# Seven half-block products for an eight-product up projection, alternating with the down projection

## The chip, the cores and the metric

The kernel runs on one core of one Trainium2 chip. The metric is device time in microseconds (us) of one execution of the whole program, as the median of several runs. In the profile PE is the matmul engine (TensorE), PEld its weight loads, DVE is VectorE, ACT ScalarE, POOL GpSimd, and SP the engine whose queue issues most transfers.

## The reference, cut to what matters

One block of a first kind is followed by two layers of a second kind. The change touches only the feed-forward of those two layers, over 512 tokens, a model width of 1024 and a hidden width of 4096, all in float32:

```
u = rms_norm(h, g_mlp) @ w_ff1              # (512, 1024) @ (1024, 4096)
h = h + jnp.square(jax.nn.relu(u)) @ w_ff2  # (512, 4096) @ (4096, 1024)
```

## The kernel before, in words

Activations are kept transposed: features on the 128 partitions, the 512 tokens along the free dimension. To keep float32 accuracy, every operand is split into a high part (rounded to the fast matmul format) and a low part (the rest), and every product is three matmuls: high x high, high x low and low x high. `xh` and `xl` are the split activations of the up product, `n.U` those of the down product.

A weight tile is 1024 rows by 256 columns (1 MB, 8 KB in each partition). SP loads the tiles in the order of `W.tiles` into `ring`, which has two slots (`NSLOT`). A load waits until both halves of the tile two places earlier have been split (`load`, L738). ACT copies a half to its high part (`high_half`, L1465), POOL subtracts to get the low part in four instructions of 128x256 (`low_half`, L2900). `wh` and `wl` hold two tiles' halves. PE's `product` (L795) makes one output tile of 128 features x 512 tokens from one half: 8 blocks of rows x 3 matmuls (L808 to L810), in one of the eight PSUM banks.

Which half is split ahead of which product is decided by `Weights.plan`: before each product it adds up to three halves whose place in `wh` and `wl` is free. Every engine then runs its own program in a fixed order; a wait at its head holds everything behind it.

The feed-forward of a layer has four groups of 1024 hidden features, each eight up products and eight down products, in the order up 0, up 1, down 0, up 2, down 1, up 3, down 2, down 3. Behind an up product DVE takes relu and the norm factor (L2574), ACT squares to the high part (L1781), DVE squares (L2576) and subtracts for the low part (L2578). Behind a down product DVE adds to `h` (L2586).

## Time and profile before

| | us |
|---|---|
| median of 3 runs | 2062.11 |
| lowest and highest | 2060.41 to 2064.62 |
| span of the profiled execution | 2057.3 |
| PE busy | 2013.4 |
| DVE, POOL, ACT busy | 1135.5, 917.4, 867.9 |

The span runs from the first to the last instruction of the program in one profiled execution. That execution's own device time is not recorded apart from it; 2062.11 less 2057.3 leaves 4.8 us around the span. A busy matmul is a pipelined record: neighbouring ones overlap, so the pace is read from their start times and not from their durations. The other engines' records are real stretches of work, save that the next may start some 0.08 us before the last one ends.

### The profile page before, as it was taken

The page shows a single profiled execution, that of the slowest core. Times are in us where ns is not written, and L with a number is a line of the kernel's source. Part 1 is how long each engine was busy: PE and PEld are TensorE (multiplying, and loading weights), DVE is VectorE, ACT ScalarE, POOL GpSimd, SP SyncE. Part 2 cuts the span into 40 slices and gives each one's busy share as a digit, 9 for nine tenths or more (in the row PEclk, how much of TensorE's full clock was granted, in tenths as well). Part 3 has the DMA queues.
Part 4 walks back from the last instruction along what each step waited for, and adds up shares of the span by engine and source line. Part 5 has one row for each costly group of instructions (what it writes and reads, how often), then busy time and mean ns, then how long its engine had stood idle before and what let it go on. Part 6 is the DMA issues. An engine that isn't in the chain of part 4 may idle for free.

```text
span 2057.3 us, 26250 instructions
## 1 busy us (share of the span) xinstructions
PE 2013.4 (98%) x10148; PEld 1574.5 (77%) x10148; DVE 1135.5 (55%) x2020; ACT 867.9 (42%) x1381; POOL 917.4 (45%) x1157
## 2 busy tenths in 40 slices
PE   6999999999999999999999999999999999999998
PEld 2877676888888767768888888786776788888877
DVE  5366758988393579955522231466996543222235
ACT  4542434443233556784322222445578532222242
POOL 1344205876566325541555555302355155555540
PEclk9999999999999999999999999999999999999999
DMA  9034631322323211103333323322111332332331
GB/s 328 25 108 143 217 123 50 105 94 80 121 84 102 89 42 42 62 21 123 92 103 103 99 86 103 102 69 83 42 42 42 103 97 98 103 103 83 102 102 62
DMA packets 188299, 194.26 MB, mean 94 GB/s; under 512 B 8592, under 2 KB 184080, under 8 KB 187792
## 3 DMA queue, kind: packets, MB, share of 16 engines
q1 hardware_dynamic: 187600, 189.44, 28.5%
q10 hardware_dynamic: 576, 3.15, 0.4%
q8 instruction: 81, 1.33, 0.3%
q14 instruction: 42, 0.34, 0.1%
HBM read 190.48 MB, written 2.10 MB: 94 GB/s over the span
## 4 chain that ended last, share of the span: by engine, by line
PE 88%; DVE 6%; POOL 2%; ACT 2%; DMA 1%; issue 1%; SPq 0%; DVEq 0%; ACTq 0%; POOLq 0%
PE ps L808 20%; PE ps L810 20%; PE ps L809 20%; PE ps L827 3%; PE ps L829 3%; PE ps L828 3%; PE ps L855 2%; POOL wl L2900 1%; DVE mix L2512 1%; PE ps L844 1%; PE ps L845 1%; PE ps L846 1%; PE ps L1355 1%; PE ps L1428 1%; PE ps L1411 1%; PE ps L1374 1%
## 5 line engine op out<-in xcount | busy, mean ns | idle before, releaser
L2900 POOL TENSOR_TENSOR wl<-ring,wh 128x256 fp32r<-128x256 f32 x1008 | 754.2, 783 | 807.5 <-ACT wh L1465 807.2
L1465 ACT ACTIVATE wh<-ring 128x1024 fp32r<-128x1024 f32 (+1 forms) x298 | 309.0, 1044 | 311.1 <-PE ps L810 256.9
L808 PE MATMUL ps<-xh,wh 128*128 128x512 f32 (+1 forms) x976 | 383.1, 393 | 2.6 <-POOL wl L2900 2.6
L810 PE MATMUL ps<-xh,wl 128*128 128x512 f32 (+1 forms) x976 | 380.6, 390 | 0.0
L809 PE MATMUL ps<-xl,wh 128*128 128x512 f32 (+1 forms) x976 | 380.6, 390 | 0.0
L808 PE MATMUL ps<-acts,wh 128*128 128x512 f32 x880 | 343.5, 390 | 0.7 <-POOL wl L2900 0.4
L810 PE MATMUL ps<-acts,wl 128*128 128x512 f32 x880 | 342.4, 389 | 0.0
L809 PE MATMUL ps<-acts,wh 128*128 128x512 f32 x880 | 342.4, 389 | 0.0
L2512 DVE SCALAR_TENSOR_TENSOR mix<-ps,par,mix 128x441 f32<-128x441 f32 (+2 forms) x352 | 213.7, 687 | 29.3 <-ACT mix L1712 29.3
L808 PEld LDWEIGHTS ps<-xh,wh 128*128 128x128 f32 (+1 forms) x976 | 183.0, 188 | 47.0 <-issue 9.1
L810 PEld LDWEIGHTS ps<-xh,wl 128*128 128x128 f32 (+1 forms) x976 | 183.0, 187 | 39.4
L809 PEld LDWEIGHTS ps<-xl,wh 128*128 128x128 f32 (+1 forms) x976 | 182.9, 187 | 38.9 <-issue 0.7
L808 PEld LDWEIGHTS ps<-acts,wh 128*128 128x128 f32 x880 | 165.2, 188 | 37.5 <-issue 3.1
L809 PEld LDWEIGHTS ps<-acts,wh 128*128 128x128 f32 x880 | 165.2, 188 | 34.5 <-issue 0.2
L810 PEld LDWEIGHTS ps<-acts,wl 128*128 128x128 f32 x880 | 165.2, 188 | 34.4
L2586 DVE TENSOR_TENSOR h<-h,ps 128x512 f32<-128x512 f32 x64 | 44.0, 688 | 254.2 <-PE ps L810 254.2
L1781 ACT ACTIVATE acts<-mix 128x512 fp32r<-128x512 f32 x64 | 40.5, 632 | 235.0 <-DVE mix L2574 235.0
L2574 DVE SCALAR_TENSOR_TENSOR mix<-ps,arena_f 128x512 f32<-128x512 f32 x64 | 44.2, 690 | 147.3 <-PE ps L810 147.3
L827 PE MATMUL ps<-xh,wh 128*128 128x512 f32 x224 | 92.9, 415 | 0.0
L1470 ACT ACTIVATE arena_m<-ps 128x512 f32<-128x512 f32 (+4 forms) x150 | 66.5, 485 | 62.0 <-PE ps L855 25.5
L829 PE MATMUL ps<-xh,wl 128*128 128x512 f32 x224 | 87.7, 391 | 0.0
L828 PE MATMUL ps<-xl,wh 128*128 128x512 f32 x224 | 87.4, 390 | 0.0
(443 smaller groups left out, 3031.4 us busy)
## 6 DMA issues: line engine op xcount, KB each, us to landing
ring<-in_w_ff_dram SPq DMA_DIRECT2D x64, 1024.0 KB, 5.2
ring<-in_w_in_dram SPq DMA_DIRECT2D x28, 1024.0 KB, 5.0
ring<-in_ffn_w_up_dram SPq DMA_DIRECT2D x22, 1024.0 KB, 4.9
ring<-in_w_ada_dram SPq DMA_DIRECT2D x17, 1024.0 KB, 5.0
ring<-in_w_out_dram SPq DMA_DIRECT2D x12, 1024.0 KB, 5.1
ring<-in_ffn_w_down_dram SPq DMA_DIRECT2D x8, 1024.0 KB, 5.0
ring<-in_w_ple_gate_dram SPq DMA_DIRECT2D x8, 1024.0 KB, 5.0
early<-in_w_ada_dram SPq DMA_DIRECT2D x7, 1024.0 KB, 10.8
```

What stands on the lines that cost most here:

```text
L808: t.matmul(b[0:m, 0:n], s.hi[:, k, a:a + m], x2[0][:, k, :], start=k == ks[0], stop=False)
L809: t.matmul(b[0:m, 0:n], s.hi[:, k, a:a + m], x2[1][:, k, :], start=False, stop=False)
L810: i = t.matmul(b[0:m, 0:n], s.lo[:, k, a:a + m], x2[0][:, k, :], start=False, stop=k == ks[-1])
L827: t.matmul(b[:, :], s.hi[:, k, a:a + 128], x2[0][:, k, :], start=k == ks[0], stop=False)
L828: t.matmul(b[:, :], s.hi[:, k, a:a + 128], x2[1][:, k, :], start=False, stop=False)
L829: i = t.matmul(b[:, :], s.lo[:, k, a:a + 128], x2[0][:, k, :], start=False, stop=k == ks[7])
L1465: a.activation(s.hi[:, :, c], s.ap[:, :, c], ACT.Copy).then_inc(*up("hi", "hi", name, hf))
L1470: a.activation(o, ps(key)[:, :] if i is None else i, func, **kw).then_inc(*free(key))
L2512: k = v.scalar_tensor_tensor(o, grid(ps(key)[:, :], dr, dc, True), pc("ffn_conv_w", w * 44 + col), o, ALU.mult, ALU.add)
L2574: v.scalar_tensor_tensor(u, ps(key)[:, :], 0.0, n.rs2, ALU.max, ALU.mult).then_inc(*free(key))
L2586: v.tensor_tensor(h[:, j, :], h[:, j, :], ps(key)[:, :], ALU.add).then_inc(*free(key))
L2900: i = p.tensor_tensor(s.lo[:, k:k + 2, c], s.ap[:, k:k + 2, c], s.hi[:, k:k + 2, c].bitcast(F32), ALU.subtract)
```

## The change

The first up group of each layer stays as it is. In the other three groups, the 1024 x 256 weights of output tiles i and i+4 are laid out on the host as a 2 x 2 of blocks: half of the rows x one output tile. The activations are a 2 x 2 of half of the rows x half of the tokens. The product of these two 2 x 2 matrices is made with seven block products in place of eight, which needs sums and differences of the blocks on both sides. A block product (a part) is 4 blocks of rows x 3 matmuls of 256 columns.

The four sums of activations are made once for each layer, during the first up group (`turned`). The sums of weights are made for each tile by DVE, in place in the ring slot, in three steps (`sums`): step 2 from the loaded tile, step 3 once the low part of part 0 is made, step 4 once that of part 1 is. The low parts of parts 1 and 4 are DVE's, the other five POOL's. The results come out in four banks, which DVE combines behind parts 2, 4 and 6 (ACT copies bank 0 out first). The order becomes: up group 0, then for each of the first three down groups four times "seven parts, two down products", then down group 3. `wh` and `wl` are now eight places, of which a seven tile takes seven and a down tile four.

The planner's rule, followed for this order, puts the splits of a pair in these places: the high copies of parts 4, 5 and 6 ahead of part 0; both halves of the down tile ahead of part 4; part 0 of the next tile ahead of part 5; part 1 of it, with steps 2 and 3 of its sums, ahead of part 6; its parts 2 and 3 ahead of the first down product; step 4 ahead of the second.

```diff
+SEVEN_RAW = (0, 1, None, 0, 1, 3, 2)
+SEVEN_X = ((0, 0), (1, 0), 1, 2, (1, 1), 3, 0)
+SEVEN_BANK = ((0, 0), (1, 0), (1, 1), (2, 0), (2, 1), (3, 0), (3, 1))
+SEVEN_WHO = ("pool", "vec", "pool", "pool", "vec", "pool", "pool")
+SEVEN_SUMS = (2, 3, 4)
+SEVEN_SUM_OF = {2: 2, 3: 3, 4: 4, 6: 2}
...
+        if seven:
+            t.parts = 7
+        n = 8 if seven else 4 * split
+        t.places = [(self.place + i) % 8 for i in range(n)] if split else [self.place % 8]
+        self.place += n
...
+            spots = self.named[name].spots(hf)
+            self.before[name, hf] = sorted({held[x] for x in spots if x in held} - {(name, hf)}, key=order.index)
+            held.update({x: (name, hf) for x in spots})
...
+                soon = first[name] < n
+                self.sum_at.setdefault(self.uses[n - soon][0], ([], []))[soon].append((name, hf))
...
+                        for p in range(b.parts):
+                            e.wait_ge(*at("lo", b.name, p))
...
+                        (q, u), x, bank = SEVEN_BANK[p], SEVEN_X[p], (*name, "bank", SEVEN_BANK[p][0])
+                        use((*name, p), name, (p,), who="pool")
+                        if u == 0:
+                            take(bank, keep=True, where=None)
+                        b = ps(bank)[:, 256 * u:256 * u + 256]
+                        e.wait_ge(*at("lo", name, p))
+                        if type(x) is int:
+                            e.wait_ge(*at("suml", l, x))
+                            x2 = n.sums[x]
+                        else:
+                            x2 = [y[:, 4 * x[0]:4 * x[0] + 4, 256 * x[1]:256 * x[1] + 256] for y in (xh, xl)]
+                        for k in range(4):
+                            hi, lo = [y[:, 128 * k:128 * k + 128] for y in (s.hi[p], s.lo[p])]
+                            t.matmul(b, hi, x2[0][:, k, :], start=k == 0, stop=False)
+                            t.matmul(b, hi, x2[1][:, k, :], start=False, stop=False)
+                            j = t.matmul(b, lo, x2[0][:, k, :], start=False, stop=k == 3)
+                        j.then_inc(*(full(bank) if q == 0 or u else up("used", "used", *name, p)))
+                        if q == 0 or u:
+                            banks.drop(bank)
+
...
+                for g in range(3):
+                    for i in range(4):
+                        seven(g + 1, i)
+                        down(g, 2 * i)
+                        down(g, 2 * i + 1)
+                for j in range(8):
...
+                for b in W.before[name, hf]:
+                    e.wait_ge(*over(W.through[b][0]))
+                if s.seven and hf in SEVEN_SUM_OF:
+                    e.wait_ge(*at("sum", name, SEVEN_SUM_OF[hf]))
+                a.activation(s.high[hf], s.raw[hf], ACT.Copy).then_inc(*up("hi", "hi", name, hf))
...
+                def seven(g, i):
+                    name = ("ff1", l, g, i)
+                    for p in range(7):
+                        high((*name, p))
+                        if p == 0:
+                            if (g, i) != (1, 0):
+                                e.wait_ge(*taken(("ff1", l, *((g, i - 1) if i else (g - 1, 3)), "bank", 1)))
+                            out_of((*name, "bank", 0), n.copied, ps((*name, "bank", 0))[:, 0:256])
+                    for u in range(2):
+                        j = i + 4 * u
+                        e.wait_ge(*at("relu", l, g, j))
+                        if j == 0:
+                            e.wait_ge(*(at("suml", l, 3) if g == 1 else done(("ff2", l, g - 2, 7))))
+                        a.activation(n.U[g % 2][0][:, j, :], n.uu[2 * (i % 2) + u], ACT.Square).then_inc(*up("act", "u2h", l, g, j))
...
+            def sums(name, p):
+
+                s = W.named[name]
+                q = s.quarter
+                if p == 2:
+                    e.wait_ge(*at("load", name))
+                    v.tensor_tensor(q[2], q[2], q[3], ALU.add).then_inc(*up("vec"))
+                    if name in W.seven_before:
+                        e.wait_ge(*at("lo", W.seven_before[name], 2))
+                    after()
+                    v.tensor_tensor(s.raw[2], q[2], q[0], ALU.subtract).then_inc(*up("vec", "sum", name, 2))
+                elif p == 3:
+                    e.wait_ge(*at("lo", name, 0))
+                    after()
+                    v.tensor_tensor(q[0], q[3], s.raw[2], ALU.subtract).then_inc(*up("vec", "sum", name, 3))
+                else:
+                    e.wait_ge(*at("lo", name, 1))
+                    after()
+                    v.tensor_tensor(q[1], q[1], s.raw[2], ALU.subtract).then_inc(*up("vec", "sum", name, 4))
 
...
+                def square_low(g, j, u):
+                    e.wait_ge(*at("u2h", l, g, j))
+                    v.tensor_tensor(u, u, u, ALU.mult).then_inc(*up("vec"))
+                    after()
+                    v.tensor_tensor(n.U[g % 2][1][:, j, :], u, n.U[g % 2][0][:, j, :].bitcast(F32), ALU.subtract).then_inc(*up("vec", "u2", l, g, j))
...
+                    for p in range(7):
+                        low((*name, p))
+                        if p == 2:
+                            e.wait_ge(*taken((*name, "bank", 0)))
+                            v.tensor_tensor(two(ua), two(bank(1)), twice(n.copied), ALU.add).then_inc(*free((*name, "bank", 1)))
+                        elif p == 4:
+                            b = bank(2)
+                            e.wait_ge(*taken((*name, "bank", 1)))
+                            v.tensor_tensor(two(n.third), two(b), twice(ua[:, 256:512]), ALU.add).then_inc(*free((*name, "bank", 2)))
+                        elif p == 6:
+                            b = bank(3)
+                            e.wait_ge(*taken((*name, "bank", 2)))
+                            v.tensor_tensor(two(ub), two(b), twice(n.third[:, 0:256]), ALU.add).then_inc(*up("vec"))
+                            v.tensor_tensor(ua[:, 256:512], b[:, 256:512], n.third[:, 256:512], ALU.add).then_inc(*free((*name, "bank", 3)))
+                            e.wait_ge(*taken((*name, "bank", 3)))
+                            for u, x in enumerate((ua, ub)):
+                                v.scalar_tensor_tensor(x, x, 0.0, n.rs2, ALU.max, ALU.mult).then_inc(*up("vec", "relu", l, g, i + 4 * u))
+                    for u, x in enumerate((ua, ub)):
+                        square_low(g, i + 4 * u, x)
...
+                if s.seven:
+                    d.dma_start(s.ap, s.srcs[0]).then_inc(*up(f"slot{s.i % NSLOT}", "load", s.name, by=16))
+                    return
...
+def blocks(w):
+
+
+    v = w.reshape(2, 4, 128, w.shape[1] // 1024, 2, 4, 128)
+    return v.transpose(3, 5, 2, 4, 0, 1, 6).reshape(w.shape[1] // 1024, 4, 128, 2048)
```

The seven tiles are now one contiguous run of 8 KB for each partition in DRAM, in place of eight runs of 1 KB. `down` is the old down product, one j at a time, on every engine. `low` on DVE makes the low parts planned for a product and then its late sums. ACT's issue of the load of `n.pT` (512 KB, ahead of the gate that follows the feed-forward) moves from behind up group 0 to behind the last seven tile.

## Rows read from the trace of the kernel before

**Rows 1.** The page: the busy line, and the chain that ended last by engine.
```profile
PE 2013.4 (98%) x10148; PEld 1574.5 (77%) x10148; DVE 1135.5 (55%) x2020; ACT 867.9 (42%) x1381; POOL 917.4 (45%) x1157
...
PE 88%; DVE 6%; POOL 2%; ACT 2%; DMA 1%; issue 1%; SPq 0%; DVEq 0%; ACTq 0%; POOLq 0%
```
**Rows 2.** Windows, layer 0's feed-forward: stretch, length, busy us (instructions) PE, PEld, DVE, ACT, POOL, clock.
```profile
978.90:1319.00 340.10, 339.65 (x1498) 279.61 (x1497) 104.63 (x143) 93.93 (x114) 187.06 (x248) 1.00 0.31 98
```
**Rows 3.** Timeline, PE, up group 1: start us, duration us, instruction. Two instructions 24 matmuls apart.
```profile
1199.89 0.39 PE L809 MATMUL ps<-xl,wh 128*128 128x512 f32 x1
...
1205.33 0.39 PE L809 MATMUL ps<-xl,wh 128*128 128x512 f32 x1
```
**Rows 4.** Timeline, PE, a product of 256 columns: two instructions 51 matmuls apart.
```profile
1489.77 0.28 PE L844 MATMUL ps<-wh,xh 128*128 128x256 f32 x1
...
1495.89 0.28 PE L844 MATMUL ps<-wh,xh 128*128 128x256 f32 x1
```
**Rows 5.** Timelines of DVE, ACT and POOL behind one up product.
```profile
1196.46 0.69 DVE L2574 SCALAR_TENSOR_TENSOR mix<-ps,arena_f 128x512 f32<-128x512 f32 x1 [2.63 <-PE ps L810]
1197.85 0.69 DVE L2576 TENSOR_TENSOR mix<-mix 128x512 f32<-128x512 f32 x1 [0.70 <-ACT acts L1781]
1198.58 0.69 DVE L2578 TENSOR_TENSOR acts<-mix,acts 128x512 fp32r<-128x512 f32 x1
...
1197.19 0.63 ACT L1781 ACTIVATE acts<-mix 128x512 fp32r<-128x512 f32 x1 [3.86 <-DVE mix L2574]
1197.73 1.05 ACT L1465 ACTIVATE wh<-ring 128x1024 fp32r<-128x1024 f32 x1
...
1198.85 3.10 POOL L2900 TENSOR_TENSOR wl<-ring,wh 128x256 fp32r<-128x256 f32 x4 [2.34 <-ACT wh L1465]
```
**Rows 6.** Timeline, DVE: a subtraction of 1024 columns.
```profile
1320.21 1.23 DVE L2014 TENSOR_TENSOR wl<-ring,wh 128x1024 fp32r<-128x1024 f32 x1 [1.32 <-ACT wh L1465]
```
**Rows 7.** Timelines of POOL and DVE while POOL works without a pause, and with pauses.
```profile
988.06 14.20 POOL L2900 TENSOR_TENSOR wl<-ring,wh 128x256 fp32r<-128x256 f32 x16 [11.28 <-ACT wh L1465]
...
1241.12 2.82 POOL L2900 TENSOR_TENSOR wl<-ring,wh 128x256 fp32r<-128x256 f32 x4 [2.56 <-ACT wh L1465]
...
989.78 1.25 DVE L2576 TENSOR_TENSOR mix<-mix 128x512 f32<-128x512 f32 x1 [0.70 <-ACT acts L1781]
991.07 1.10 DVE L2578 TENSOR_TENSOR acts<-mix,acts 128x512 fp32r<-128x512 f32 x1
992.10 0.68 DVE L2574 SCALAR_TENSOR_TENSOR mix<-ps,arena_f 128x512 f32<-128x512 f32 x1
```
**Rows 8.** The chain around a late weight half: start us, us, what.
```profile
338.87 0.25 PE ps L1170
...
339.20 1.07 ACT wh L1465
...
340.34 2.81 POOL wl L2900 x4
...
343.29 0.47 PE ps L808
```
**Rows 9.** The issue of a tile load on SP's queue; a load in the chain and its reader.
```profile
1202.03 0.37 SPq L751 DMA_DIRECT2D ring<-in_w_ff_dram  x1
...
168.21 5.35 DMA ring<-in_w_in_dram
173.59 1.07 ACT wh L1465
```
**Rows 10.** The page's transfers: KB each, median us from issue to landing.
```profile
ring<-in_w_ff_dram SPq DMA_DIRECT2D x64, 1024.0 KB, 5.2
...
mix<-in_p_dram ACTq DMA_DIRECT2D x2, 512.0 KB, 3.5
```
**Rows 11.** Windows as in rows 2, last column GB/s: long rows (4 to 8 us), 1 KB rows.
```profile
4.00:8.00 4.00, 0.00 (x0) 0.00 (x0) 0.00 (x0) 0.00 (x0) 0.00 (x0) 1.00 1.00 421
16.00:20.00 4.00, 3.94 (x18) 1.09 (x18) 1.77 (x3) 0.00 (x0) 0.00 (x0) 1.00 1.09 386
```

More of the change, by code:

```diff
@@ L414, in build @@
         wh_t, wl_t = sb("wh", 2 * SLOT, F32R), sb("wl", 2 * SLOT, F32R)
+        with ExitStack() as low:
+            sb("beside", 2048, where=low)
+            sum3 = sb("sum3", 2048, F32R, where=low)
         mix_t, ring = sb("mix", 4096), sb("ring", NSLOT * SLOT)
@@ L455, in done, with over @@
             return (f"full{b}", handles[f"full{b}"]), n + 1
+        def over(key):
+            if key[0] != "ff1" or len(key) < 5:
+                return done(key)
+            q, u = SEVEN_BANK[key[4]]
+            return done((*key[:4], "bank", q)) if q == 0 or u else at("used", *key)
         def taken(key):
@@ L560, in build @@
             with ExitStack() as low:
+                with ExitStack() as high:
+                    sum0 = sb(f"sum0{l}", 2048, F32R, where=high)
                 cut = Cut(sb(f"arena_f{l}", 3072, where=low), 3072)
@@ L565, in build @@
                     a1 = sb(f"acts{l}1", 8192, F32R, where=high)
+                    sum1, sum2 = [sb(f"sum{i}{l}", 2048, F32R, where=high) for i in (1, 2)]
+                with ExitStack() as high:
+                    plain = sb(f"plain{l}", 5120, where=high)
                 with ExitStack() as high:
@@ new lines, in down @@
+                def down(g, j):
+                    product(("ff2", l, g, j), ("ff2", l, g, j // 2), j % 2, n.U[g % 2], xk=("u2", l, g), who="pool")
+                    if g == 3 and j == 4:
+                        take(("parts", ("p", l)), keep=True)
+                for jl in range(8):
+                    product(("ff1", l, 0, jl), ("ff1", l, 0, jl // 2), jl % 2, (xh, xl), xk=("xl", ("m", l)), who="pool", keep=jl < 2)
+                    if jl == 0:
+                        row_squares(("m", l), b, n.sq2)
+                        banks.drop(("parts", ("m", l)))
+                    if jl == 1:
+                        fold(("var", ("m", l)), ("parts", ("m", l)), n.part)
+                        for i in range(2):
+                            banks.drop(("ff1", l, 0, i))
@@ new lines, in down @@
+                def down(g, j):
+                    high(("ff2", l, g, j))
+                    if g == 3:
+                        feed(("p", l), j, taken(("ff2", l, 3, j)), ("g_ple_2", l), n.sq2, n.U[0][0], done(("ff2", l, 2, 7)))
+                for jl in range(8):
+                    if jl >= 4:
+                        turned(jl - 4)
+                    if jl != 1:
+                        high(("ff1", l, 0, jl))
+                    if jl == 0:
+                        rows_of(("parts", ("m", l)), n.part)
+                        high(("ff1", l, 0, 1))
+                        root(("m", l), n.rs2)
+                    e.wait_ge(*taken(("ff1", l, 0, jl)))
+                    e.wait_ge(*done(("wo", l, 7)))
+                    a.activation(n.U[0][0][:, jl, :], n.uu[jl % 4], ACT.Square).then_inc(*up("act", "u2h", l, 0, jl))
@@ L2598, in vector @@
+                for g in range(3):
+                    for i in range(4):
+                        seven(g + 1, i)
+                        down(g, 2 * i)
+                        down(g, 2 * i + 1)
                 for k in range(2):
```

269 lines of the change are left out of this document (137 added, 132 removed).

## The prediction

> **What bounds the kernel now.** I read the page's busy line and its chain first: PE is busy for 98% of the span and carries 88% of the chain, no other engine more than 6% [rows 1]. Then the windows of the stage that changes: in 340.10 us of layer 0's feed-forward PE is busy for 339.65, while DVE has 104.63 and POOL 187.06 [rows 2]. So PE alone sets the pace there, and fewer PE cycles would show in full, as long as nothing else becomes late. That is the question, since the change gives the other engines more to do for every product.
>
> **PE: what is removed and added.** Matmuls overlap, so the pace is the distance of starts. With 512 columns 24 matmuls take 5.44 us, 0.227 each, across a product's boundary too [rows 3]. With 256 columns 51 take 6.12 us, 0.120 each [rows 4]: half the columns cost more than half the time. Removed are two up products, 2 x 5.44 = 10.88 us. Added are 7 parts x 12 x 0.120 = 10.08 us. The saving is 0.80 us for each pair of output tiles, not an eighth of 10.88. There are 4 pairs x 3 groups x 2 layers = 24, so PE's work shrinks by 19.2 us. A pair with its two down products takes PE 20.96 us where it took 21.76.
>
> **What has to fit beside it.** By counts nothing is near its limit. POOL has 10 + 8 instructions of 0.70 (four in 2.82 us [rows 7]), 12.6 of 20.96 us. DVE has 17 of 0.69 and one of half the size, about 12.1. ACT has seven copies of 512 columns at 0.63, two of 1024 at 1.05, two squares at 0.63 and one copy of 256 columns, about 8.2 [rows 5]. But a seven tile is worked on in its ring slot, so its slot comes free only when the last low part (part 6) is made, and then the next seven tile is loaded. That makes a loop: load, split, sums, split, load. A wait now stands at the head of DVE ahead of part 6's results: DVE makes the next tile's low part 1 and sums 2 and 3 first, and behind these are queued bank 3, both relus, ACT's squares, DVE's four squares and subtractions, the add of the first down product, and only then sum 4, for which the high copy of part 4 and, in ACT's order, those of 5 and 6 wait.
>
> I follow that loop from the landing, T = 0. Hand-offs are 0.03 us from ACT to DVE, 0.04 from DVE to ACT, 0.08 from ACT to POOL, 0.04 between dependent DVE operations [rows 5]; where nothing is waited for, the next DVE operation starts about 0.08 before the end of the last [rows 7]. One thing is not in the counts: a DVE operation with two SBUF operands and a POOL subtraction don't run side by side. With POOL working without a pause, L2576 takes 1.25 and L2578 1.10 in place of 0.69, and POOL's 16 take 14.20 where 11.2 would do, but L2574, which reads PSUM, keeps 0.68 [rows 5, 7]. They take turns, a turn of 0.61 for DVE and 0.70 for POOL. The values then are:
> - ACT copies parts 0 and 1, to 0.65 and 1.18. POOL has the turn for part 0 from 0.73; DVE's low part 1 gets it at 1.42, POOL's second at 2.03, DVE's sum 2 at 2.72 and, its second half, at 3.45; sum 3 ends at 4.87.
> - Bank 3 from 4.79: one operation of 512 and one of 256 columns (no row; 1024 take 1.23 and 512 take 0.69 [rows 5, 6], so 0.42), to 5.81. Relus to 6.54 and 7.15. ACT squares to 7.21 and 7.82, then copies parts 2 and 3. DVE squares and subtracts the first tile to 8.66, POOL takes its turn with part 2, and the second tile's two operations begin at 9.27 and 10.57. The add starts at 11.18 and sum 4 at 11.87, to 12.56.
> - ACT copies parts 4, 5, 6, to 13.22, 13.75, 14.28. POOL has four instructions for parts 5 and 6 from 13.83, to 16.65.
>
> The reload comes on top. From POOL's end to SP's issue is 0.08 [rows 5, 9], from landing to the reader 0.03 [rows 9]. A tile with 1 KB rows takes 5.2 us to land, up to 5.35 in the chain [rows 9, 10]. The seven tile has 8 KB rows. Below, 512 KB land in 3.5 [rows 10], and at 421 GB/s [rows 11] the other 512 KB add 1.25: 4.75. I take 4.9, between, and keep 4.75 and 5.35. The loop is 0.11 + 4.9 + 16.65 = **21.65 us**, over PE's 20.96. The port waits in it are 2.2 us; with none it is 19.4, and with a full wait of 0.56 (1.25 less 0.69) on all eleven SBUF-only operations 25.6. I take my count, since each wait in it is a meeting of two named operations.
>
> The Trainium skill (DMA: Bandwidth & Descriptors, section "Anatomy of one DMA — SWDGE (gpsimd) path") fits a transfer as 2.0 us plus bytes over 436,000 per us. By that a tile would land in an estimated 4.4 us, against 5.2 on this kernel's SP queue [rows 10], and the loop would be 21.15.
>
> How does PE wait? POOL makes the down tile's first half behind part 6's low part: four instructions, 2.78, and 0.14 more to PE with 0.07 for its restart (POOL ends at 343.15, PE starts at 343.29 [rows 8]), then 10.88 of down products: 13.9 from the end of part 6's low part to the end of the pair. Even with POOL free, ACT's copy of that half waits for part 3's end (ACT starts 0.33 after the start of a last matmul of 0.23 [rows 8], so 0.10 past the product's end): 5.76 + 0.10 + 1.07 + 0.07 + 2.82 + 0.14 = 9.96 [rows 7, 8], just inside 10.08. In the first pair the last products of up group 0, behind which `turned` puts four subtractions of 1024 columns (1.23 each), delay part 6's low part to about 8.0 us; the bounds are 4.7 (DVE and ACT free) and 8.6 (when PE wants it). A layer's 12 pairs take 8.0 + 11 x 21.65 + 13.9 = 260.1 us against 12 x 21.76 = 261.1. Both layers: 2 x (-1.1) = **-2.1 us**. Each 0.1 us of the loop is worth 2.2 us.
>
> **Edits that I cost at nothing.** ACT's four copies of sums and DVE's small operations for them fall into up group 0, where DVE is busy about 2.1 of each 5.44 us [rows 5]; uncovered, the copies of 1.05 alone would be 8.4 us in both layers. The load of `n.pT`, moved on ACT's queue, lands in 3.5 [rows 10] and is first waited for after the last seven tile, with 10.88 us of down products still ahead of down group 3; uncovered, 3.5 each. The 864 added matmuls bring waits at the parts' boundaries; rows 4 cross such boundaries at full pace. SP's issues stay in order, and the down tile's slot is free before the next pair's load is due. The clock stays at 1.00 [rows 2], the 2.4 GHz level.
>
> **The sum.** It is made against the span of 2057.3, which has 4.8 us around it up to the median 2062.1. 2057.3 - 2.1 = 2055.2, so the median becomes **2060.0**.
>
> **Rivals.**
> *PE sets the pace.* The loop fits into 20.96 us: a landing at 4.75 and one port wait less (0.56) do it. Then all of PE's saving shows: 2062.1 - 19.2 = 2043. For it: POOL and DVE have enough free time by count. Against it: every wait in my chain stands in the program's order.
> *A quicker landing.* Long rows land half a microsecond sooner than I take, in 4.4. Loop 21.15, 22 x 0.5 = 11 us better than the forecast: 2049. For it: 421 against 386 GB/s [rows 11]; against it: no 1 MB load of the trace is as quick. The fit of the Trainium skill quoted above gives this case.
> *Slower: the loop is over 21.8.* The mechanism is the slot's turnaround with the port shared by DVE and POOL: a landing of 5.3 (+0.4) and part of another turn lost (+0.15) make 22.2 us, and 22 x 0.55 - 2.1 = +10 us: 2072. It is slower by more than 0.2% from a loop of 21.93 on. For it: the 1.25 and 1.10 of rows 7, and that one more collision costs 0.56; against it: my chain has its collisions in already.
> *It doesn't do what it says.* The slot isn't what the loop turns on, because the sums wait for something that I read wrongly, and time stays at 2062.
>
> **Chances.** Forecast 0.43 (loop 21.4 to 21.95, 2054.5 to 2066.6), PE sets the pace 0.15, quicker landing 0.13, slower 0.25, nothing as it says 0.04. A measurement of this kernel can tell about 0.2% (4.1 us) from no change. Faster by more: 0.15 + 0.13 + 0.11 of the forecast's case (loop under 21.56) = 0.39. Within: 0.28 + 0.04 = 0.32. Slower: 0.25 + 0.04 = 0.29. The forecast's own range is 2054 to 2067; the range of 8 in 10 reaches from PE's pace, 2043, to 2074, just over the slower case.
>
> **What the profile after would show.** 256-column matmuls 0.120 us apart. If the loop holds: PE idle of about 0.7 us in each pair, just ahead of the first down product, released by POOL's low part; pairs 21.6 to 21.7 us apart; part 6's low part ending about 7.8 us into its pair; DVE's low part 1 waiting for ACT, and that for the load. A SBUF-only DVE operation of 1.1 to 1.3 beside POOL. A load landing in 4.75 to 5.0. If PE sets the pace, pairs are 20.96 apart and PE has no such idle time. I am wrong in kind if PE waits at a part's matmuls for a sum or for a bank, or if DVE's low part 1 doesn't wait for the load.

## The result, and the profile after

The changed kernel takes **2067.0 us** (median of 9 runs, 2065.87 to 2070.24) against 2059.05 us of the kernel before (9 runs, 2057.09 to 2064.62). The ratio is 1.0038, 95% interval 1.0028 to 1.0048. It is slower, by about 8 us; I had forecast 2 us less than before. The profiled execution has a span of 2065.2 us, 7.9 more than before. Its time is 1.8 us above its span, as in most runs of either kernel (2.2 at most), and not the 4.8 that I had put around the span of the kernel before: the median of three runs that I started from stood 3 us above that of nine. On this footing my forecast of 2060.0 reads 2057.0.

The page of the changed kernel, busy us (share of the span) and instructions, its chain that ended last by engine, and the landing of the tiles that feed a seven (KB each, median us):

```profile
PE 2004.0 (97%) x11012; PEld 1604.4 (78%) x11012; DVE 1348.8 (65%) x2302; ACT 924.8 (45%) x1533; POOL 987.8 (48%) x1205
...
PE 83%; DVE 10%; POOL 3%; ACT 2%; DMA 1%; issue 1%; SPq 0%; DVEq 0%; ACTq 0%; POOLq 0%
...
ring<-in_ff_seven_dram SPq DMA_DIRECT2D x24, 1024.0 KB, 4.8
```

PE is busy for 9.4 us less than in [rows 1], and yet the span is longer: PE now stands idle somewhere, and DVE has 10% of the chain where it had 6%. Two windows say where. The first is layer 0's feed-forward, which answers to [rows 2]; the second is seven of its twelve pairs (columns as there):

```profile
978.23:1322.71 344.48, 334.77 (x1928) 294.19 (x1927) 210.30 (x284) 122.28 (x189) 222.51 (x272) 1.00 0.28 97
...
1085.28:1233.36 148.08, 148.07 (x925) 134.00 (x924) 90.63 (x126) 50.95 (x83) 101.74 (x126) 1.00 0.29 100
```

The stage takes 344.48 us where it took 340.10 between the corresponding instants, and PE is idle in it for 9.7 us. In these seven pairs PE is never idle: they take 148.08 us, 21.15 each. So most of the idle time stands ahead of them. PE's waits from 978 to 1045 us (in all, times, longest):

```profile
PE ps L864 <- POOL wl L3068: 3.5, 2, 3.2
PE ps L1304 <- POOL wl L3068: 2.3, 1, 2.3
PE ps L1304 <- DVE wl L2107: 1.6, 1, 1.6
PE ps L1304 <- issue: 1.2, 1, 1.2
```

And where they stand in PE's timeline (start, duration, instruction, idle before it and what ended that):

```profile
1008.59 0.47 PE L864 MATMUL ps<-xh,wh 128*128 128x512 f32 x1 [3.21 <-POOL wl L3068]
...
1016.56 0.36 PE L1304 MATMUL ps<-xh,wh 128*128 128x256 f32 x1 [2.26 <-POOL wl L3068]
...
1023.85 0.36 PE L1304 MATMUL ps<-sum,wh 128*128 128x256 f32 x1 [1.25 <-issue]
...
1027.07 0.39 PE L1304 MATMUL ps<-xh,wh 128*128 128x256 f32 x1 [1.56 <-DVE wl L2107]
```

These are the last product of up group 0, the start of the first seven, and two of its parts (a fifth wait of 0.29 us stands ahead of the down product behind it): the handover from whole products to sevens. Measured against a full pace of 0.227 and 0.120 us a matmul, PE loses 11.3 us between 979 and 1040 us, and the same 11.3 in layer 1; 0.2 of each belong to the change of width that every pair has. I call this figure the loss of the handover, and give it for the experiments too, from the start of up group 0 to the start of the second seven. The wait that the trace puts down to issue, at part 3, ends 0.1 us behind POOL's low half for that part (from 1020.98, 2.77 us long). What the other engines do there is shown by their timelines. DVE's:

```profile
987.75 0.83 DVE L2682 TENSOR_SCALAR plain<-h,par 128x256 f32<-128x256 f32 x1
...
992.96 0.68 DVE L2756 SCALAR_TENSOR_TENSOR mix<-ps,arena_f 128x512 f32<-128x512 f32 x1
...
1000.88 0.69 DVE L2756 SCALAR_TENSOR_TENSOR mix<-ps,arena_f 128x512 f32<-128x512 f32 x1
...
1003.60 1.22 DVE L2691 TENSOR_TENSOR plain<-plain 128x1024 f32<-128x1024 f32 x1
1004.73 1.76 DVE L2694 TENSOR_TENSOR sum<-plain,sum 128x1024 fp32r<-128x1024 f32 x1
```

ACT's:

```profile
1001.60 0.63 ACT L1879 ACTIVATE acts<-mix 128x512 fp32r<-128x512 f32 x1 [6.34 <-DVE mix L2756]
```

And POOL's:

```profile
1004.20 4.25 POOL L3068 TENSOR_TENSOR wl<-ring,wh 128x256 fp32r<-128x256 f32 x4 [5.35 <-ACT wh L1541]
```

Read it from below. PE's wait at 1008.59 ends with POOL's low half (1004.20, 4.25 us long). POOL waited 5.35 us for ACT's copy of those weights, which in ACT's order stands behind the square L1879 and behind ACT's own copy of a sum (1.04 us), and ACT had waited 6.34 us for DVE's result L2756 of 1000.88. DVE had waited for nothing but ACT's squares, 0.70 us each: it was making `turned`'s sums, eight operations in 5.2 us (987.75 to 992.96), eight more from 995.67 to that result, and then the subtractions of 1024 columns. My forecast priced all of this at nothing.

### The profile page after: what moved, and what is told of

It is laid out like the page before. It is cut to its first block, busy times and chain, and to the rows that moved or that the text cites. A ratio compares the mean times of both kernels' runs of the same rounds, so it can differ in the third digit from the quotient of the medians.

```text
span 2065.2 us, 28721 instructions
## 1 busy us (share of the span) xinstructions
PE 2004.0 (97%) x11012; PEld 1604.4 (78%) x11012; DVE 1348.8 (65%) x2302; ACT 924.8 (45%) x1533; POOL 987.8 (48%) x1205
## 4 chain that ended last, share of the span: by engine, by line
PE 83%; DVE 10%; POOL 3%; ACT 2%; DMA 1%; issue 1%; SPq 0%; DVEq 0%; ACTq 0%; POOLq 0%
PE ps L864 15%; PE ps L866 15%; PE ps L865 15%; PE ps L1305 3%; PE ps L1306 3%; PE ps L1304 3%; PE ps L883 3%; PE ps L885 3%; PE ps L884 3%; POOL wl L3068 2%; PE ps L911 2%; DVE mix L2624 1%; PE ps L900 1%; PE ps L901 1%; PE ps L902 1%; PE ps L1430 1%
## 5 line engine op out<-in xcount | busy, mean ns | idle before, releaser
L1541 ACT ACTIVATE wh<-ring 128x1024 fp32r<-128x1024 f32 (+3 forms) x394 | 338.3, 888 | 308.0 <-DMA ring<-in_ff_seven_dram 93.8
L864 PE MATMUL ps<-xh,wh 128*128 128x512 f32 (+1 forms) x592 | 234.2, 396 | 9.0 <-POOL wl L3068 9.0
L866 PE MATMUL ps<-xh,wl 128*128 128x512 f32 (+1 forms) x592 | 231.1, 390 | 0.0
L865 PE MATMUL ps<-xl,wh 128*128 128x512 f32 (+1 forms) x592 | 231.1, 390 | 0.0
L2107 DVE TENSOR_TENSOR wl<-ring,wh 128x512 fp32r<-128x512 f32 (+2 forms) x92 | 89.9, 980 | 134.3 <-ACT wh L1541 134.3
L864 PEld LDWEIGHTS ps<-xh,wh 128*128 128x128 f32 (+1 forms) x592 | 110.9, 187 | 39.4 <-issue 16.3
L866 PEld LDWEIGHTS ps<-xh,wl 128*128 128x128 f32 (+1 forms) x592 | 110.9, 187 | 24.4
L865 PEld LDWEIGHTS ps<-xl,wh 128*128 128x128 f32 (+1 forms) x592 | 111.0, 187 | 23.7 <-issue 0.7
L1304 PE MATMUL ps<-sum,wh 128*128 128x256 f32 x384 | 108.9, 284 | 2.8 <-issue 2.5
L1305 PE MATMUL ps<-sum,wh 128*128 128x256 f32 x384 | 108.6, 283 | 0.0
L1306 PE MATMUL ps<-sum,wl 128*128 128x256 f32 x384 | 108.5, 283 | 0.0
```

Of the source, the lines that this page charges most:

```text
L864: t.matmul(b[0:m, 0:n], s.hi[:, k, a:a + m], x2[0][:, k, :], start=k == ks[0], stop=False)
L865: t.matmul(b[0:m, 0:n], s.hi[:, k, a:a + m], x2[1][:, k, :], start=False, stop=False)
L866: i = t.matmul(b[0:m, 0:n], s.lo[:, k, a:a + m], x2[0][:, k, :], start=False, stop=k == ks[-1])
L1304: t.matmul(b, hi, x2[0][:, k, :], start=k == 0, stop=False)
L1305: t.matmul(b, hi, x2[1][:, k, :], start=False, stop=False)
L1306: j = t.matmul(b, lo, x2[0][:, k, :], start=False, stop=k == 3)
```

## The experiments

The theory from this reading: **the preparation of the sums (`turned`) in up group 0 makes DVE late, and everything behind it**; the pairs run at PE's own pace. The rivals: the ring slot's loop sets the pace of the pairs, as I had forecast; the alternating order costs by itself; ACT's order, not DVE's load, makes the weights late.

### The preparation left out

```
-                            e.wait_ge(*at("suml", l, x))
-                            x2 = n.sums[x]
+                            x2 = [y[:, 0:4, 0:256] for y in (xh, xl)]
...
-                    turned(jl)
```

> The changed kernel without the four sums of activations (turned on ACT and DVE); the parts that used them read a plain block instead, so part of the computation is left out. Theory: DVE's work for these sums in up group 0 makes the square and the weight copies behind it late, and the five waits of PE from the 7th product of up group 0 to the first down product (3.4, 2.4, 1.4, 1.7, 0.4 us in layer 0) come from it. Then nearly all of 9.4 us for each layer goes: about 2067 - 18 = 2049 us, and the pairs stay 21.16 apart. Rival: the first seven tile's own chain (weight sums 2 to 4 and six low parts behind the last products of group 0) is too long by itself; then only the first wait goes, about 2060.

Parts 2, 3, 5 and 6 of a seven read a plain block of the input in place of its sums here, so that part of the computation is changed. Measured: 2046.7 us (2043.86 to 2048.21), ratio 0.9935 (0.9921 to 0.9949). From 978 to 1045 us the trace lists no wait of PE at all. The loss of the handover is 0.1 us in both layers. So the preparation costs 20 us, it costs them in the handovers, each of which loses 11.2 us less, and without it the sevens are worth 12 us over the kernel before. This run leaves out DVE's and ACT's share of the preparation together. DVE's timeline of this run shows why the room was smaller than I had thought:

```profile
991.08 0.68 DVE L2752 SCALAR_TENSOR_TENSOR mix<-ps,arena_f 128x512 f32<-128x512 f32 x1
992.46 1.25 DVE L2696 TENSOR_TENSOR mix<-mix 128x512 f32<-128x512 f32 x1 [0.70 <-ACT acts L1876]
993.74 1.10 DVE L2698 TENSOR_TENSOR acts<-mix,acts 128x512 fp32r<-128x512 f32 x1
994.77 0.68 DVE L2752 SCALAR_TENSOR_TENSOR mix<-ps,arena_f 128x512 f32<-128x512 f32 x1
...
1003.30 0.69 DVE L2752 SCALAR_TENSOR_TENSOR mix<-ps,arena_f 128x512 f32<-128x512 f32 x1 [1.09 <-PE ps L866]
```

A product occupies DVE for 3.69 us while POOL works (991.08 to 994.77), the pause for ACT's square in it, and not for 2.1. And the first result that has to wait for PE is the one at 1003.30: until then DVE is catching up on the reciprocal, which is 3.35 us long and waits for the norm's square root on ACT (L1597 in the changed kernel); it starts at 978.92 in the changed kernel and at 982.25 in this run. Even without the preparation DVE is behind for half of up group 0.

### The results ahead of the next tile's last part

```
                     for p in range(7):
-                        low((*name, p))
+                        if p < 6:
+                            low((*name, p))
...
                                 v.scalar_tensor_tensor(x, x, 0.0, n.rs2, ALU.max, ALU.mult).then_inc(...)
+                            low((*name, 6))
```

> The changed kernel with one thing moved on DVE: behind part 6 it first takes bank 3 and makes both relus, and then the next tile's low part 1 and sums 2 and 3. Theory: the loop through the ring slot sets the 21.16 us of a pair. Without about 2.4 us in it the loop is no bound, PE's last wait ahead of the down products goes, and a pair takes 20.96 to 21.05: 22 x 0.15 = 3 us faster, about 2064, with part 6's low part ending near 5 us into the pair instead of 7.1. Rival: PE's own pace with its changes of width makes the 21.16; then part 6's low part ends earlier just as well but pairs stay at 21.16 and the time at 2067.

Measured: 2067.54 us (2066.18 to 2067.8), ratio 1.0035 (1.0022 to 1.0049), where the rival had 2067; pairs of 21.12 us. The slot's turn is now decoupled from the pace, as PE's and SP's timelines of this run show: the load of a seven tile is issued 6.05 us after the start of a seven (1085.87 and 1091.92), where it was 7.2 us in the changed kernel (1085.28 and 1092.46), and the pairs are as long as they were within 0.04 us.

```profile
1085.87 0.28 PE L1304 MATMUL ps<-xh,wh 128*128 128x256 f32 x1
...
1106.99 0.28 PE L1304 MATMUL ps<-xh,wh 128*128 128x256 f32 x1
```

```profile
1091.92 0.34 SPq L801 DMA_DIRECT2D ring<-in_ff_seven_dram  x1
```

That the time is not lower all the same has another reason. The first seven takes 16.4 us where it took 14.8, and the handover loses 12.7 us instead of 11.3, since the granted clock fell lower and twice (windows; the last three columns are clock, DMA share, GB/s):

```profile
1008.00:1012.00 4.00, 4.00 (x10) 3.13 (x11) 3.27 (x5) 1.21 (x3) 0.00 (x0) 0.50 0.75 248
1024.00:1028.00 4.00, 3.19 (x15) 2.90 (x15) 2.94 (x4) 3.62 (x6) 3.09 (x4) 0.50 0.00 0
```

The order is not what does this: with the same order the run that combines it with 1 KB rows (below) loses 11.3 us in layer 0 and 13.0 in layer 1, and the 1 KB rows with the old order lose 11.3 and 12.7.

### The seven's tiles in rows of 1 KB

```
-                    d.dma_start(s.ap, s.srcs[0]).then_inc(...)
+                    d.dma_start(s.ap.rearrange("p (k n) -> p k n", k=8),
+                        s.srcs[0].rearrange("(k p) n -> p k n", p=128)).then_inc(...)
```

> The changed kernel with the seven tiles laid out in DRAM in runs of 1 KB, eight for each partition, as the other tiles. Theory of the loop: landing goes from 4.8 to 5.1 us, and every pair becomes 0.2 to 0.3 us longer, 21.4: 22 x 0.25 = 5.5 us slower, 2072. Rival (PE's own pace): landing 5.1, pairs 21.16, 2067.

Measured: 2077.68 us (2074.86 to 2079.21), ratio 1.0084 (1.0071 to 1.0097), more than the 2072 that I expected. The landing is 5.3 us instead of 4.8, and the pairs grow to 21.5 us. The page's row of the loads, and PE's timeline:

```profile
ring<-in_ff_seven_dram SPq DMA_DIRECT2D x24, 1024.0 KB, 5.3
```

```profile
1085.15 0.28 PE L1304 MATMUL ps<-xh,wh 128*128 128x256 f32 x1
...
1106.63 0.28 PE L1304 MATMUL ps<-xh,wh 128*128 128x256 f32 x1
...
1117.25 0.47 PE L864 MATMUL ps<-acts,wh 128*128 128x512 f32 x1 [0.35 <-issue]
```

PE now waits 0.35 us ahead of the down product. So the loop that I had forecast is real, but it is shorter than I had counted: in the changed kernel it fits under PE's pace, with so little to spare that 0.5 us more in the landing shows as 0.35 to 0.4 us in each pair.

### 1 KB rows and the results first, together

Both edits above.

> Edit: e3_rows_1k (the seven's tiles in runs of 1 KB, landing 5.3 instead of 4.8 us) and e2_results_first (the last low half of a seven does not wait behind the results of the tile before, so the slot is free 1.1 us earlier after the seven's start: 6.05 instead of 7.2 us) together. If the ring's loop took over the pace in e3_rows_1k (pair 21.16 -> 21.6 us) and stands about 0.1 us short of it in the changed kernel, the earlier slot pays for the longer landing: pairs of 21.16 us again and the time of e2_results_first, 2067 to 2069. If the longer landing costs pace for another reason (more packets, contention with the down tiles), the pairs stay at 21.5 to 21.6 us and the time at 2076 to 2079.

Measured: 2067.64 us (2066.03 to 2072.51), ratio 1.0050 (1.0036 to 1.0063). The landing is 5.3 us again, and the pairs are back at 21.12 us, as PE's timeline shows:

```profile
1083.93 0.28 PE L1304 MATMUL ps<-xh,wh 128*128 128x256 f32 x1
...
1105.05 0.28 PE L1304 MATMUL ps<-xh,wh 128*128 128x256 f32 x1
```

The 10 us of the 1 KB rows came by way of the loop: freeing the slot earlier gave them back, with the longer landing still there. This settles what sets the pairs' pace: PE, at 21.12 to 21.16 us.

### The order alone

```
-                up2(0)
-                up2(1)
-                down2(0)
...
+                for what, g, j in FF_ORDER:
+                    (up2 if what == "ff1" else down2)(g, (j,))
```

> The kernel before with the new order alone: two ordinary up products alternate with two down products. Expected by every theory of mine: no wait of PE, as each half has the same 5.44 us, so 2059 as before. If the alternation itself costs (a wait for the squares at the head of a down group, or a late load), it shows here as waits at group heads.

This is the kernel before, with two up products and two down products in turn as the changed kernel has its pairs. Measured: 2058.73 us (10 runs, 2056.99 to 2062.03), ratio 0.9997 (0.9988 to 1.0006). The order is free.

### ACT's weights first

```
+                    if 1 <= jl <= 4:
+                        high(("ff1", l, 0, jl + 1))
                     if jl >= 4:
                         turned(jl - 4)
-                    if jl != 1:
+                    if jl >= 6:
                         high(("ff1", l, 0, jl))
```

> Edit: in up group 0 the ScalarE copies the next weight half (products 2 to 5) before the square of the present product instead of behind it; nothing else moves. If the first handover wait (TensorE idle 3.60 us before 1008.59) stands because ScalarE's copy of the weights is queued behind a square that waits for a late result, it goes from both layers: 2067.3 - 2 x 3.4 = 2060.5, and the waits of the first seven (1016.56 to 1031.93, about 6 us a layer) stay. If VectorE's late result holds TensorE by itself (a bank is not freed in time), the wait stays and the time is 2066 to 2068.

Measured: 2067.42 us (2065.56 to 2068.02), ratio 1.0037 (1.0023 to 1.0051), where I expected 2060.5. The wait at the last product of up group 0 is gone as expected, but my figure for the time fell: the next one grew from 2.26 to 5.7 us, as this run's waits of PE show.

```profile
PE ps L1304 <- POOL wl L3071: 5.7, 1, 5.7
```

The loss of the handover is 11.2 us. The wait had only been passed on. The path through ACT's queue is the one the trace names, and still it isn't the cause; behind the first place stands a second one where DVE's lateness is collected: POOL waits there for ACT's next copies, which stand behind the square of a result that DVE makes only at 1011.49.

### One row of blocks for each product

```
-                    if jl in (2, 3):
-                        for j in (0, 1) if jl == 2 else (2, 3):
+                    if jl < 4:
+                        for j in (jl,):
```

> Edit: the smallest one, one row of blocks at each of products 0 to 3 instead of two rows at products 2 and 3, still ahead of the product's own result; all else as in the changed kernel. If bunching alone counts, the late results at products 2 and 3 go, and with them the waits at 1008.59 and most of that at 1016.56 (about 5 us a layer); those of the 1024-column subtractions (1023.85 to 1031.93, about 3.7 us a layer) stay: 2067.3 - 10 = about 2057.5 (2055 to 2060). If the place ahead of the result counts as well, the waits fall by less than half: 2062 to 2066.

Measured: 2064.58 us (10 runs, 2061.46 to 2068.42), ratio 1.0026 (1.0017 to 1.0035). The wait at the last product halves (a start 1.78 us after the last one, instead of 3.60), the others stay as they were. The handovers lose 9.5 us instead of 11.3; the ratio's interval still overlaps that of the changed kernel. The gain is less than bunching alone would give, and is what I had expected if the place ahead of the result counts as well.

### The preparation spread and behind the results

```
-                    turned(jl)
...
                     square_low(0, jl, u)
+                    turned(jl)
...
+                    for x in {5: (1,), 6: (2, 3), 7: (0,)}.get(jl, ()):
```

> Edit: the preparation of the sums is spread over up group 0: one row of blocks (four operations of 256 columns) at each of products 1 to 4 instead of two rows at products 2 and 3, the subtractions of 1024 columns at 5, 6, 6, 7, all of it queued behind the product's own result and square on VectorE and ScalarE instead of ahead of them. The work is the same, only its place differs. Theory of bunching (VectorE has about 3.3 us idle of each product's 5.44, some 26 us in the group, for 14 to 18 us of preparation, but two rows ahead of a result make it 6 us late): the five handover waits of a layer, about 9.4 us, fall to under 1.5 us, time 2067.3 - 2 x 8.5 = about 2050 (2047 to 2053). Rival, the amount: VectorE and POOL slow each other whenever the preparation runs, wherever it stands; then the waits move within the group and the time stays at 2060 to 2067.

Measured: 2072.06 us (2067.18 to 2075.18), ratio 1.0054 (1.0041 to 1.0068), where I expected 2050: no faster than the changed kernel, and by its handovers (12.9 and 14.5 us) rather slower. My theory of bunching fell. DVE's timeline in this run:

```profile
1015.66 1.75 DVE L2693 TENSOR_TENSOR sum<-plain,sum 128x1024 fp32r<-128x1024 f32 x1
1017.34 1.21 DVE L2115 TENSOR_TENSOR ring<-ring 128x512 f32<-128x512 f32 x1
...
1019.79 0.69 DVE L2123 TENSOR_TENSOR ring<-ring,arena_f 128x512 f32<-128x512 f32 x1
1020.39 0.68 DVE L2754 SCALAR_TENSOR_TENSOR mix<-ps,arena_f 128x512 f32<-128x512 f32 x1
```

Here the subtractions run straight into the sums of the first seven's weights (1017.34 to 1020.39), and the result behind them is late again. Wherever the work is put between the reciprocal and the first seven, DVE has no room for it. An estimate from the rows shown: reciprocal 3.35, eight products at 3.69, part 1 and the weight sums of the first seven 4.1 (1017.34 to 1020.39 and another operation of 1.0), four rows of blocks at 2.6, five operations of 1024 columns at 1.1 to 1.7: about 54 us of work and pauses in eight products of 5.44, 43.5 us. About 10 us are over, and the changed kernel lost 11.3.

With the order of the second experiment added:

> Edit: the spread of g1_spread_late and the order of e2_results_first together. In e2_results_first the seven at 1233 lost no time where the changed kernel lost 0.9 us a layer, and paid about 1.3 us more at the first seven, where the sums came late. With the sums early this second cost has no reason left: g1's time less 1.8 us, about 2048 (2046 to 2051). Rival: the order of part 6 and the results costs at the first seven for its own reason: then it is no faster than g1_spread_late.

Measured: 2068.94 us (2067.65 to 2069.72), ratio 1.0045 (1.0032 to 1.0057), where I expected 2048. In this text, and again in that of h2 below, I took a loss of 0.9 us at 1233 us for a property of each layer. It isn't: it is one load that took 5.88 us to land, in one layer only, and the run without the preparation has one of 6.0 at another place. With the results first the slot comes free 1.1 us earlier, and late loads cost nothing: neither one of 6.53 us in the second experiment nor one of 7.51 in this run lengthens a pair.

### The plain sums in DVE's idle stretch

```
-                    if jl in (2, 3):
-                        for j in (0, 1) if jl == 2 else (2, 3):
+                    if jl == 0:
+                        for j in range(4):
...
-                    elif jl >= 4:
+                    elif jl in (2, 3, 4, 5):
```

> Edit: the seventeen operations that form the plain sums (sixteen of 256 columns and one of 1024) are queued on VectorE at product 0 of up group 0 ahead of the reciprocal (L2238), where VectorE stands idle for 10.95 us in the changed kernel (967.97 to 978.92); ScalarE's copies and VectorE's four subtractions of 1024 columns come at products 2 to 5 instead of 4 to 7. The runs with the rows spread showed VectorE busy without a break for the last three products, the weights' own sums for the first seven (5.5 us) with it, so the theory is now: what counts is VectorE's whole load from the reciprocal to the first seven, and only work taken out of that stretch comes back. 16 x 0.48 + 1.22 = 8.9 us fit into the idle stretch; left are 4 x 1.22 us early in the group. Expected: the five handover waits under 1.5 us a layer together, 2047 to 2052, likeliest 2049, which is about 2 us over the kernel without the preparation. Rival (the reciprocal is held up, and with it the results of products 0 and 1, or POOL's part counts): 2056 to 2067.

Measured: 2051.95 us (2048.37 to 2053.4), ratio 0.9962 (0.9950 to 0.9975), inside the 2047 to 2052 that I expected and faster than the kernel before. The handovers lose 2.8 and 3.9 us. ACT's copies of the sums and DVE's subtractions stand two products earlier here as well; what this part gives by itself wasn't tried. In the changed kernel DVE waited ahead of the reciprocal:

```profile
978.92 3.35 DVE L2238 RECIPROCAL arena_f<-arena_f 128x512 f32<-128x512 f32 x1 [10.94 <-ACT arena_f L1597]
```

In this run the stretch is filled, and the reciprocal starts at 980.74, 0.6 us later than it would have without this (this run is 1.2 us behind the other in its times there):

```profile
969.08 0.35 DVE L2682 TENSOR_SCALAR plain<-h,par 128x256 f32<-128x256 f32 x1
...
980.74 3.34 DVE L2238 RECIPROCAL arena_f<-arena_f 128x512 f32<-128x512 f32 x1
```

The seventeen operations take 11.7 us there and not the 8.9 that I had counted, since POOL works beside some of them (from 969.40 and 974.49, 3.4 and 3.5 us). Two waits are left in layer 0, 2.1 us at the first seven's part 4 (`PE ps L1304 <- DVE wl L2107`), and 0.3 behind it. With the results first as well:

> Edit: h1_sums_in_the_gap with the results of a seven ahead of the next part 6 and its sums (the order of e2_results_first). If VectorE has room at the first seven, this order takes away the 0.9 us a layer lost at the sixth pair or so (1233) and costs nothing: 1 to 2 us under h1_sums_in_the_gap. Rival: the next tile's sums come later by the results' 2.5 us, and the first seven pays for it whatever the load: the same as h1 or slower by 1 to 2 us.

Measured: 2049.18 us (2047.03 to 2055.05), ratio 0.9958 (0.9944 to 0.9972). Its interval holds the ratio of the run before, so the order's own share is not shown. The handovers lose 2.9 and 3.0 us.

### The subtractions in DVE's pause

The two edits of the last run stay, and this one is added:

```
-                    turned(jl)
+                    if jl == 0:
+                        turned(jl)
...
+                    if jl:
+                        turned(jl)
                     square_low(0, jl, u)
```

> Edit: h2_gap_results_first, and the four subtractions of 1024 columns stand between a product's result and its square's two operations on VectorE, where VectorE waits 0.7 us for ScalarE's square, instead of ahead of the result. In h2_gap_results_first VectorE is busy without a break from 969 to 1013 us, late with each result from product 3 on, and the first seven still loses 2.9 us a layer (2.35 and 0.57). Four pauses of 0.7 us filled take most of it: 2 x 2 to 2 x 2.9 us off, 2044 to 2047 (h2 median 2049.2). If VectorE's load from the reciprocal on isn't what is left, the two waits stay and the time is that of h2, 2048 to 2051.

Measured: **2045.67 us** (2044.28 to 2049.15), ratio 0.9942 (0.9929 to 0.9954), as expected (2044 to 2047). Where a subtraction stands in the pause, DVE no longer waits for ACT's square:

```profile
989.46 1.22 DVE L2693 TENSOR_TENSOR sum<-plain,sum 128x1024 fp32r<-128x1024 f32 x1
990.59 1.23 DVE L2698 TENSOR_TENSOR mix<-mix 128x512 f32<-128x512 f32 x1
```

PE's waits from 978 to 1045 us:

```profile
PE ps L864 <- POOL wl L3072: 0.6, 2, 0.5
```

This row is all that is left of PE's waits from 978 to 1045 us. The first seven is 9.95 us long, as the others are, where it was 14.80, and the handovers lose 1.2 us. The whole computation is done here, in the time of the kernel without the preparation: this version beats the kernel before by 0.6%.

## Why the prediction was wrong, point by point

**What bounds the kernel: right.** PE sets the pace of the pairs [rows 1, 2]; its waits come from elsewhere.

**PE's saving: right in kind, 0.20 us a pair too high.** The matmuls are 0.120 and 0.227 us apart, as in [rows 3, 4]. But a pair takes 21.16 us, not 20.96. The rows of the changed kernel show most of it at the change of width: the first down matmul starts 0.15 to 0.20 us after the last one of 256 columns, where the pitch is 0.12, and the next one 0.30 after it, where it is 0.23.

```profile
1116.55 0.47 PE L864 MATMUL ps<-acts,wh 128*128 128x512 f32 x1
1116.85 0.39 PE L865 MATMUL ps<-acts,wh 128*128 128x512 f32 x1
```

So 24 pairs save 14.4 us, not 19.2.

**The loop of the ring slot: the mechanism is real, its size 0.5 us too large, and so it didn't bind.** I had 21.65 us. The trace of the changed kernel gives, in the timelines of SP, ACT, DVE (sum 4) and POOL:

```profile
1092.46 0.34 SPq L801 DMA_DIRECT2D ring<-in_ff_seven_dram  x1
...
1113.71 0.34 SPq L801 DMA_DIRECT2D ring<-in_ff_seven_dram  x1
```

```profile
1097.44 1.15 ACT L1541 ACTIVATE wh<-ring 128x512 fp32r<-128x512 f32 x2 [4.12 <-DMA ring<-in_ff_seven_dram]
```

```profile
1108.76 0.68 DVE L2127 TENSOR_TENSOR ring<-ring,arena_f 128x512 f32<-128x512 f32 x1
```

```profile
1110.79 5.66 POOL L3068 TENSOR_TENSOR wl<-ring,wh 128x256 fp32r<-128x256 f32 x8 [0.75 <-ACT wh L1541]
```

The chain of work from the landing at 1097.44 to the end of POOL's fourth instruction (1110.79 and half of 5.66: 1113.62) is 16.2 us, forecast 16.65: sum 4 starts 11.32 us after ACT's first copy, where I had it at 11.87, because the steps were a little shorter than I had them. DVE's squares began 0.15 us earlier; the second tile's two operations, which met POOL, took 1.23 and 1.11 us, 0.54 and 0.42 over the first tile's 0.69, where I had 0.61 each; and the add before sum 4 took 0.59 from start to start. The landing is 4.8 us, forecast 4.9. Together some 21.1. Among my rivals this is "PE sets the pace", to which I gave 0.15. Its sign of recognition, pairs without idle time of PE, is what the windows show. The estimate of 21.15 us which the Trainium skill's fit gave (DMA: Bandwidth & Descriptors, "Anatomy of one DMA — SWDGE (gpsimd) path") comes near to the measured loop, but by another landing: 4.4 us by the fit, which is for transfers that GpSimd issues, and 4.8 measured here on SP's queue. The measured landing decides.

**`turned` at nothing: the step that failed.** I wrote that it falls into up group 0, "where DVE is busy about 2.1 of each 5.44 us", and that 8.4 us would be the price uncovered. It cost 20 us. Three things were wrong in that sentence. [rows 5] show a product in the middle of the stage, with DVE's pause for ACT left out of the 2.1 and POOL idle beside it; [rows 7], which I used for the loop but not here, show the same three operations at 1.25, 1.10 and 0.68. Nor did I ask where DVE stands when the group begins: it begins with a reciprocal of 3.35 us, which makes it late from the first product on. And I priced what is uncovered by ACT's copies alone, while the work was DVE's: sixteen operations of 0.34 to 0.85 us and five of 1.2 to 1.8 in each layer. The sign that I had written down for being wrong in kind (PE waits at a part's matmuls for a sum) came true in the first seven, by way of the low half of part 3, which is made from a sum; in the pairs it did not.

**The two errors pull against each other.** The loop, which didn't bind, made the forecast 10 us too slow: without the preparation the sevens gave 12.3 us, not 2.1. The preparation at nothing made it 20 us too fast. The miss of 10 us is the difference of the two; that it is no larger is luck.

**The first pair** I had late by its part 6 at 8.0 us; in fact it was held up by its parts 0, 3 and 4, and PE's first wait stands a product earlier.

**The load of `n.pT`, the 864 matmuls, the down tile's slot** cost nothing that the trace shows, nor did the new order, by a run of its own.

**The sum as measured**, against full pace: 24 pairs at -0.60 are -14.4; two handovers at 11.1 (11.3 less the 0.2 that is in each pair's figure) are +22.2; one late landing +0.9. That is +8.7, and the spans differ by 7.9; the remaining 0.8 I haven't placed.

## What to carry to other kernels

Work that is moved beside the bounding engine is free only if the engine that does it has room in that very stretch: count its load from where it enters the stretch late to where it is next needed, with its pauses and with the durations that rows beside a busy neighbour show, not from a typical product. When a wait is named in a trace, test whether removing its immediate cause only passes it on; here it did, and the cure was to give the work a stretch where DVE had 10.9 us idle and pauses that another engine leaves. And a loop through a load that is within 0.1 us of the pace should be given room, because single loads land 1 us late and more.

## What the runs showed of the hardware

**TensorE's clock fell after its waits, and what that costs depends on what comes behind.** A window of the changed kernel, behind the waits of 3.21 and 2.26 us (the last three columns are granted clock, DMA share, GB/s):

```profile
1016.00:1020.00 4.00, 3.44 (x19) 3.47 (x20) 3.30 (x5) 1.83 (x3) 2.16 (x3) 0.68 0.01 4
```

The granted clock is 0.68 over these four us, a mixture of the levels 2.4 and 1.2 GHz, and from 1017.5 to 1020.9 us matmuls of 256 columns stand 0.213 apart instead of 0.120:

```profile
1018.54 0.41 PE L1304 MATMUL ps<-xh,wh 128*128 128x256 f32 x1
1018.75 0.41 PE L1305 MATMUL ps<-xl,wh 128*128 128x256 f32 x1
```

These 16 matmuls take 1.5 us more, and they stand inside the 11.3 us of the handover. But they don't add to it, as the run with one row of blocks for each product shows. There the clock is 0.60 in layer 0 (1016 to 1020 us) and stays at 1.00 in layer 1 (1696 to 1700 us), and the wait at part 3 makes up for it:

```profile
1024.14 0.36 PE L1304 MATMUL ps<-sum,wh 128*128 128x256 f32 x1 [1.26 <-issue]
...
1704.08 0.35 PE L1304 MATMUL ps<-sum,wh 128*128 128x256 f32 x1 [2.62 <-issue]
```

Both stand 7.28 us behind the start of their seven (1016.86 and 1696.80): the weights come late, and a slower PE only waits less for them. Where no such wait follows, the slow matmuls show in the time. In the run with the plain sums in the idle stretch PE waits 2.1 us at part 4 in both layers; in layer 1 the clock falls behind it (0.70 from 1693 to 1697 us), in layer 0 it stays at 1.00, and the first seven and its down products take 24.9 us against 23.8. In the second experiment such a fall comes behind part 3, and the first pair is 1.1 us longer than the changed kernel's.

**DVE and POOL slow each other.** While POOL works (987.41 to 990.93), an operation of 256 columns on DVE takes 0.84 us that takes 0.48 without it. The one with a single large operand takes 0.83 instead of 0.34, so that it is not only those with two SBUF operands, as I had written. A subtraction of 1024 columns takes 1.76 in place of 1.22 beside POOL at 1004.73; at 1020.80 it keeps 1.22, and it is POOL whose two instructions take 2.77. Whether the preparation would fit without this slowing was not tried: no run took POOL's work out of the stretch.

**Single loads land late**: in layer 0 of the changed kernel eleven of the twelve tiles that feed a seven land in 4.7 to 5.1 us and one in 5.88 (issued at 1219.49, read from 1225.37), in layer 1 none is late. The longest landing of such a tile in any run is 7.51 us (1838.46 to 1845.97, in the spread version with the results first). Where the loop has no room, such a load costs time: 0.9 us in the changed kernel.
